# Six matrix jobs instead of four beside the first modulation, three of them summed in SBUF, and the later modulation loads spread out

## The reference, cut to what matters

```
mod = silu(c) @ w_ada + b_ada                      # 2048 x 12288 weights, one vector
sh_a, sc_a, gt_a, sh_f, sc_f, gt_f = split(mod, 6)
h = rmsnorm(x, norm_mix) * (1 + sc_a) + sh_a       # 256 x 2048
p = h @ w_in                                       # 2048 x 9296 weights
c_q, c_kv, k_pe, q_g, k_g, v_g, z, b_logit, a_logit, gates = split(p)
...                                                # attention from c_q, c_kv, k_pe; gated delta rule
                                                   # from conv(q_g, k_g, v_g); both gated and summed
```

## Time and profile before

| | |
|---|---|
| median of 3 runs | 2292.34 us (2292.03 to 2294.39) |
| the profiled execution | 2293.58 us, span 2292.3 us |
| PE busy | 2235.2 us (98%), mean granted clock 0.996 |
| PEld busy | 1855.7 us (81%) |
| DVE busy | 1505.7 us (66%) |
| ACT busy | 1009.0 us (44%) |
| DMA | 506.75 MB, 221 GB/s over the span; 363 and 381 GB/s in the first two fortieths |

### The profile page before, as it was taken

One profiled execution on the slowest core, in us unless ns is written; L12 is line 12 of the kernel. 1 busy time (PEld: TensorE's weight loads), 2 busy tenths in 40 slices (PEclk: granted clock), 3 DMA queues, 4 the chain that ended last, 5 costly groups with the idle time before them and its releaser, 6 DMA issues.

```text
span 2292.3 us, 26935 instructions
## 1 busy us (share of the span) xinstructions
PE 2235.2 (98%) x10767; PEld 1855.7 (81%) x10767; DVE 1505.7 (66%) x1927; ACT 1009.0 (44%) x1270; POOL 24.4 (1%) x28
## 2 busy tenths in 40 slices
PE   5998999999999999999999999999999999999998
PEld 3678898888887888888888888887888888888886
DVE  5888898887768777765554555467555555555556
ACT  4345445343444464443344434456444444434444
POOL 0000000000000000000000000000000000000000
PEclk9999999999999999999999999999999999999999
DMA  9966767685678768876555565555555555555553
GB/s 363 381 240 209 245 228 258 198 271 197 220 269 307 275 239 285 273 242 202 184 192 193 184 202 184 191 195 193 191 195 188 188 188 190 187 185 194 197 189 130
DMA packets 276445, 506.75 MB, mean 221 GB/s; under 512 B 24032, under 2 KB 38112, under 8 KB 275296
## 3 DMA queue, kind: packets, MB, share of 16 engines
q1 hardware_dynamic: 276320, 505.03, 65.0%
HBM read 502.51 MB, written 2.49 MB: 220 GB/s over the span
## 4 chain that ended last, share of the span: by engine, by line
PE 82%; DVE 8%; DMA 4%; ACT 2%; issue 2%; SPq 0%; POOL 0%; DVEq 0%; ACTq 0%
PE bank L1200 25%; PE bank L1202 25%; PE bank L1201 25%; DVE WL L1927 3%; PE bank L1391 2%; DMA RAW<-in_w_o_dram 2%; DVE GA L1908 1%; PE bank L1121 1%; ACT WH L1480 1%; PE bank L1212 1%; PE bank L1214 1%; PE bank L1213 1%; DMA RAW<-in_w_o_gdn_dram 1%; PE bank L1148 1%; PE bank L1363 1%
## 5 line engine op out<-in xcount | busy, mean ns | idle before, releaser
L1927 DVE TENSOR_TENSOR WL<-RAW,WH 128x1024 fp32r<-128x1024 f32 (+1 forms) x714 | 864.9, 1218 | 619.2 <-ACT WH L1480 616.5
L1480 ACT CAST WH<-RAW 128x1024 fp32r<-128x1024 f32 (+1 forms) x714 | 743.3, 1047 | 917.6 <-PE bank L1202 733.1
L1200 PE MATMUL bank<-WH,HTh 128*128 128x512 f32 x1936 | 770.4, 398 | 7.3 <-DVE WL L1927 6.5
L1202 PE MATMUL bank<-WH,HTl 128*128 128x512 f32 x1936 | 755.9, 390 | 0.0
L1201 PE MATMUL bank<-WL,HTh 128*128 128x512 f32 x1936 | 755.5, 390 | 0.0
L1200 PEld LDWEIGHTS bank<-WH,HTh 128*128 128x128 f32 x1936 | 364.2, 188 | 88.7 <-DVE WL L1927 11.3
L1201 PEld LDWEIGHTS bank<-WL,HTh 128*128 128x128 f32 x1936 | 364.4, 188 | 77.1 <-issue 4.3
L1202 PEld LDWEIGHTS bank<-WH,HTl 128*128 128x128 f32 x1936 | 364.0, 188 | 76.5
L1908 DVE SCALAR_TENSOR_TENSOR GA<-RAW,ST,GA 128x512 f32<-128x512 f32 x264 | 181.2, 747 | 13.9 <-DMA RAW<-in_w_ada_dram 7.7
L1200 PE MATMUL bank<-WH,R2h 128*128 128x512 f32 x408 | 164.1, 402 | 3.5 <-DVE WL L1927 3.5
L1202 PE MATMUL bank<-WH,R2l 128*128 128x512 f32 x408 | 159.9, 392 | 0.0
(11 more groups left out here) (273 smaller groups left out, 1756.3 us busy)
## 6 DMA issues: line engine op xcount, KB each, us to landing
RAW<-in_a_w_in_dram SPq DMA_DIRECT2D x96, 1024.0 KB, 5.0
RAW<-in_w_gate_up_dram SPq DMA_DIRECT2D x88, 1024.0 KB, 5.0
RAW<-in_w_ada_dram SPq DMA_DIRECT2D x80, 1024.0 KB, 5.2
RAW<-in_w_in_dram SPq DMA_DIRECT2D x63, 1024.0 KB, 5.0
RAW<-in_w_down_dram SPq DMA_DIRECT2D x44, 1024.0 KB, 5.0
RAW<-in_a_w_out_dram SPq DMA_DIRECT2D x32, 1024.0 KB, 5.0
A<-in_w_ada_dram SPq DMA_DIRECT2D x16, 1024.0 KB, 11.7
RAW<-in_w_o_dram SPq DMA_DIRECT2D x16, 1024.0 KB, 5.1
```

What stands on the lines that cost most here:

```text
L1200: e.matmul(o, ah[:, s], hi[:, k, :], start=first, stop=False)
L1202: i = e.matmul(o, al[:, s], hi[:, k, :], start=False, stop=last)
L1480: e.copy(hi, rv).then_inc(S["hi"], 1)
L1927: e.tensor_tensor(lo, rv, hi.bitcast(F32), ALU.subtract).then_inc(S["lo"], 1)
```

## The change

Two more jobs run in the front: `conv` 1 (here `q1`; `conv` 0 is `q0`) and the first gate job `ga` 0. The three jobs `q0`, `q1` and `ga` 0 share banks 6 and 7. Each runs its 4 kt of the round as a group of its own, and its partial sum is then taken to SBUF: in round 0 ACT copies it to a buffer CS, in the later rounds DVE adds it there (the new step `acc`, two instructions of 128x512, which wait for the end of that group). The order within a round becomes `cq`, `q0`, `ckv`, `q1`, `sm`, `ga`, with the g units between them. The final evictions of these three jobs read CS instead of PSUM. The rule that spreads the later g units is replaced by a table: none in `conv` 2 and the seven latent units, more in `ga`, `z` and `gb`. `JX` moves to another address.

The core of the diff:

```diff
@@ make_jobs
     front = [Job("sm", ...), Job("cq", ...), Job("ckv", ...),
-             conv(0, O_Q)]
-    a1 = [conv(1, O_Q + 512), conv(2, O_K)]
+             conv(0, O_Q), conv(1, O_Q + 512), Job("ga", 0, plain(win, O_GATE), 16, 512, "ht")]
+    for n in range(3):
+        front[3 + n].acc = n
+    a1 = [conv(2, O_K)]
@@ plan_units
-            w = [("w", j, 4 * c, 4) for j in jobs[:4]]
-            u.extend([w[0]] + f[:1] + [w[1]] + f[1:5] + [w[2]] + f[5:] + [w[3]])
+            sm, cq, ckv, q0, q1, ga = (("w", j, 4 * c, 4) for j in jobs[:6])
+            u.extend([cq] + f[:1] + [q0] + f[1:2] + [ckv] + f[2:3] + [q1] + f[3:5] + [sm] + f[5:6] + [ga] + f[6:])
...
-        thick = (("conv", 3), ("conv", 4), ("og", 2), ("og", 3))
+        quarters = {"conv": (0, 0, 0, 2, 2, 3), "ga": (0, 3, 3, 3), "z": (3, 3), "gb": (3, 3, 3, 3), "og": (1, 1, 2, 2), "wo": (2, 2, 0, 0),
+                    "uqn": (0, 0), "uqp": (0,), "ukk": (0, 0), "ukv": (0, 0)}
@@ front, one round c
             self.put("mod_e", 2 * c + 1, None)
             self.put("h", c)
+            if c:
+                self.front_unit()
+                self.put("acc", 2, c - 1, acc)
             if more:
                 self.front_unit()
             self.front_unit()
+            self.front_half(cq, 0)     # twice
...
+            self.front_half(q0, 3)     # twice
+            acc = self.used
+            if more:
                 self.front_unit()
             self.front_unit()
+            self.put("acc", 0, c, acc)
+            self.front_half(ckv, 1)    # twice
+            if more:
+                self.front_unit()
+            self.front_half(q1, 3)     # twice
+            acc = self.used
+            if more:
+                self.front_unit()
+            self.front_unit()
+            self.put("acc", 1, c, acc)
+            if more:
+                self.put("mod_e", 2 * c + 2, None)
+                self.put("cam", c + 1)
+                self.front_unit()
+            else:
+                self.put("rope_tables")
+            self.front_unit()
+            if more:
                 self.front_unit()
                 self.front_unit()
+            self.front_half(sm, 2)     # twice
+            self.front_half(ga, 3)     # twice
+            acc = self.used
+        self.put("acc", 2, 3, acc)
@@ pe_program, half
+            group = j.nkt if j.acc is None else 4
...
-                first, last = kt == 0, kt == j.nkt - 1
+                first, last = kt % group == 0, kt % group == group - 1
@@ act_program
+        elif kind == "acc" and args[1] == 0:
+            n, _, done = args
+            W.wait_ge("half", done)
+            for q in range(2):
+                e.copy(L.CS[n][:, 512 * q:512 * q + 512], bank[6 + q]).then_inc(S["acc_a"], 1)
@@ dve_program
+        elif kind == "acc" and args[1]:
+            n, c, done = args
+            W.wait_ge("half", done)
+            W.wait_ge(*acc_event(n, c - 1))
+            for q in range(2):
+                total = L.CS[n][:, 512 * q:512 * q + 512]
+                e.tensor_tensor(total, bank[6 + q], total, ALU.add).then_inc(S["acc_d"], 1)
```

More of the change, by code:

```diff
@@ L461, in front @@
         self.issue_loads()
-        where = {"cq": 0, "ckv": 1, "conv": 3, "sm": 2}
+        sm, cq, ckv, q0, q1, ga = jobs
         for ci in range(2):
@@ L482, in front @@
             self.front_unit()
-            for j in (jobs[0], jobs[1]):
-                self.front_halves(j, where[j.name])
-            for _ in range(4 * more):
+            self.front_half(cq, 0)
+            self.front_half(cq, 0)
+            if more:
+                self.front_unit()
+            else:
+                latent = self.done(cq, 0)
+                next(latent)
+            self.front_unit()
+            self.front_half(q0, 3)
+            if not more:
+                next(latent)
+            self.front_half(q0, 3)
+            acc = self.used
+            if more:
                 self.front_unit()
             self.front_unit()
-            self.front_halves(jobs[2], where[jobs[2].name])
+            self.put("acc", 0, c, acc)
+            self.front_half(ckv, 1)
+            if not more:
+                next(latent, None)
+            self.front_half(ckv, 1)
+            if more:
+                self.front_unit()
+            self.front_half(q1, 3)
+            self.front_half(q1, 3)
+            acc = self.used
[6 more added lines that the diff above has]
+                self.put("cam", c + 1)
+                self.front_unit()
+            else:
+                self.put("rope_tables")
+            self.front_unit()
             if more:
@@ L518, in front_unit, with front_half @@
         self.issue_loads()
-    def front_halves(self, j, where):
-        for _ in range(2):
-            self.put("half", self.used, where)
-            self.used += 1
+    def front_half(self, j, where):
+        assert self.halves[self.used][0] is j
+        self.put("half", self.used, where)
+        self.used += 1
         j.end = self.used
@@ L779, in q_rest, with first_convs @@
         self.have.add("qpt")
+    def first_convs(self):
+        for n in range(2):
+            for i in range(2):
+                self.put("conv", n, i, None)
+                yield
+            self.bg.append(self.conv_rest(n))
+            yield
+            yield
     def conv_rest(self, n):
@@ L1188, in pe_program @@
                 b, pr = (bank[2 * where], bank[2 * where + 1]), (where,)
-            if t0 == 0 and tiles[0] == 0:
+            group = j.nkt if j.acc is None else 4
+            if t0 % group == 0 and tiles[0] == 0:
                 for n in pr:
@@ L1218, in pe_program @@
                 i.then_inc(S["tile"], 1)
-            if t0 + nk == j.nkt:
+            if (t0 + nk) % group == 0:
                 for n in pr:
-                    held[n] = evicted(j)
+                    held[n] = evicted(j) if j.acc is None else [acc_event(j.acc, t0 // 4)]
         elif kind == "lat_t":
@@ L1598, in act_program @@
                 W.wait_ge(*RAW1_FREE[1])
-            W.wait_ge("half", job_end(sch, "conv", n))
+            if n < 2:
+                W.wait_ge(*acc_event(n, 3))
+                u = [L.CS[n][:, 512 * q:512 * q + 512] for q in range(2)]
+            else:
+                W.wait_ge("half", job_end(sch, "conv", n))
+                u = [bank[2 * pr], bank[2 * pr + 1]]
             W.wait_ge("nat_t", 2 * n - 2)
@@ L1653, in act_program @@
             W.wait_ge("att_lo", 8)
-            W.wait_ge("half", job_end(sch, kind, c))
+            if (kind, c) == ("ga", 0):
+                W.wait_ge(*acc_event(2, 3))
+                u = [L.CS[2][:, 512 * bb:512 * bb + 512] for bb in range(2)]
+            else:
+                W.wait_ge("half", job_end(sch, kind, c))
+                u = [bank[2 * pr], bank[2 * pr + 1]]
             d = L.M if kind == "ga" else L.GB
             for bb in range(2):
-                e.activation(d[:, bb, 512 * c:512 * c + 512], bank[2 * pr + bb], ACT.Tanh, scale=0.5
+                e.activation(d[:, bb, 512 * c:512 * c + 512], u[bb], ACT.Tanh, scale=0.5
                              ).then_inc(S[kind], 1)
```

47 lines of the change are left out of this document (27 added, 20 removed).

## The result

The changed kernel takes 2365.99 us (2365.71 to 2368.9, 4 runs) against 2293.36 us (2292.03 to 2294.58, 4 runs) beside it: ratio 1.0319, 95% interval 1.0306 to 1.0332. It is slower, as forecast, but by 73 us where 39 were forecast, and 2366 is outside the range of 2312 to 2350.

A forecast was written before the change was run, and what follows sets the result against it. It took DMA to bound the front, DVE the stage behind, TensorE 340 to 680 us. Front stalls 38.7, clock +9, small waits -1, stage behind -10, stage after +2 gave +38.7 us: 2331 us, range 2312 to 2350.

The forecast's parts named there:

- The chain behind `q1`: In the front, PE waits for DVE's ordered work after the group of `q1`; stalls together 38.7 us (36.5 to 40).
- The bounds on an `acc`: DVE's adding step in the front was taken as 1.4 us, between 1.1 and 1.5 us.
- The clock: PE runs at half clock after each long front stall: 9 us taken, 5 to 17 possible.
- Small waits in the front: PE's earlier mid-round gaps for g units in the front go: -1 us (-3 to 0).
- rival 1: Front runs as its loads say, PE's 5.8 us lack there gone: -14 us, 2278 us; chance 6%.
- The stage behind the front: From 155.6 to 340 us before, fewer g units relieve DVE and PE waits less: -10 us (-16 to 0).
- on average PE leads: Behind the front, some 129 us of DVE work would stand against 148 us of PE work.
- The stage after it: 340 to 680 us: 11 more g units in `b1`, 30 us of DVE, cost PE +2 us (0 to +10).
- Rival 3: DVE becomes the bound in `b1` on top of the front's stalls: +62 us, 2354 us; chance 9%.

The follow-up runs named there:

- the third kernel: Changed kernel with only the front reordered: g units, `mod_e` and rope tables ahead of the `acc` they stood behind; new table kept; 2316.71 us.
- kernels 1 and 2: First: changed kernel with the old g-unit rule, `gb` 0 and 1 thick, 2358.76 us; second: kernel before with the new table alone, 2300.3 us.
- Kernel 6 against 5: Five front jobs, reordered front, old rule, `gb` 0 thick: 6 has `conv` 1 there without `ga` 0, 2310.03 us; 5 the reverse, 2301.81 us.
- Kernel 9: `kp` put two slots later, against six front jobs in the reordered front with the old g-unit rule (2312.27 us); 2312.25 us.
- kernel 8: VectorE's taps on `conv` 0 and 1 narrowed to 16 columns, against six jobs, reordered front, old rule (2312.27 us); 2306.55 us.
- kernels 10 and 11: `ga` 3 instead of `ga` 2 without g units: 10 with six jobs and `kp` later, 2307.58 us; 11 with five jobs including `ga` 0, 2295.46 us.
- kernel 7: Six jobs, reordered front, new table with three g units moved from `ga` 2 and 3 to `conv` 4, 5 and `gb` 0; 2314.35 us.

## Why the prediction was wrong, point by point

The forecast was +38.7 us, and the two steps that failed are its terms for what comes behind the front: -10 for the stage behind it and +2 for the stage after that. Measured, they are +6.7 and +27.5 us. The front was 7.8 us cheaper than forecast, which hid part of it.

**The chain behind `q1`: right.** Forecast 11.0 us in rounds 1 and 2, 7.2 in round 0, 6.9 in round 3, 2.6 at the end, 38.7 in all. The trace has 10.7 twice, 7.3, 6.7 and 2.5 (PE in order of time; the first two of them):

```profile
80.22 3.78 PE L1201 MATMUL bank<-GA,CST 128*128 128x512 f32 x4 [7.25 <-DVE GA L1982]
...
132.73 3.78 PE L1201 MATMUL bank<-GA,CST 128*128 128x512 f32 x4 [10.67 <-DVE GA L1982]
```

An `acc` took 1.29 us, within its bounds of 1.1 to 1.5. Rounds took 50.5, 53.6 and 52.3 us; 53 was forecast. (The bounds on an `acc`, which stands in four of the five sums, give 37.5 to 39.1, not 36.5 to 40.)

**The clock: right in kind, a little less.** The account has 9.7 us of slow clock in the front against 2.6 before, so 7.1 where 9 was taken. The forecast's lower end of 5 came from no row (five stalls at 1.7 us are 8.5). The front of after has 41 us at half clock; 9.7 us lost to it means that some 20 of them had PE at work, and the others lay within the waits, where they cost nothing. The Trainium skill ("TensorE: Matmul & The Clock Gate", section "Loop structure matters more than you think") has VectorE's copy out of PSUM as something that does not break PE's warmth where the next matmuls follow at once. The traces agree with that condition: in the third kernel, with the same `acc` beside matmuls that go on, the clock is full from 46.4 to 227.3 us; in after PE stood for VectorE, and the clock fell to half at each long wait.

**Small waits in the front: too small.** Forecast -1 us (-3 to 0). Before lost 18.5 us to `conv` 2, 2.6 of it by the clock, so 15.9 by waits; after has 57.4 - 9.7 = 47.7, of which 37.8 are the five named. That leaves 9.9, 6.0 less, of which 2.0 with its clock are `conv` 1's own, lost behind the front before. The prediction had such a sum itself, as the 5.8 us in rival 1, but not in the main sum. `conv` 2 so began at 240.84 us, not at 247.

**The stage behind the front: the first step that failed.** Forecast -10 us (-16 to 0), measured 24.7 - 18.0 = +6.7 (+4.7 if `conv` 1's 2.0 us are counted here, as the prediction did). The waits for VectorE that were to become fewer went from 15.3 to 18.1 us, and the slow clock from 2.8 to 6.6. The part on g units was right: kernels 1 and 2 show the table worth -11 to -13 us there. (By the rule in `plan_units` 17 g units stood in `a1`, two of them in `conv` 1, where 18 and four were counted; that is 2.7 us of VectorE and moves no term.) What failed is the other half of the sentence, that `conv` 1's 23 us of PE work go and only 9.4 us of splits with them, so that "on average PE leads". The average was the wrong measure. The jobs from `conv` 2 to `conv` 3 have beside them the taking out of `conv` 0, `conv` 1, `conv` 2, both latents and `sm`'s gates (PE loses 17.9 us there, 9.9 before), and VectorE was already nearly full there before, 43.65 of 46.9 us from `uqn` 0 to `conv` 3 (the kernel before, columns as above):

```profile
212.50:259.40 46.90, 43.63 (x281) 39.42 (x282) 43.65 (x71) 25.16 (x36) 4.22 (x4) 0.96 0.82 238
```

`conv` 1's PE work was the cover for that. Kernel 6 against 5 prices it at 20 us, of which the table hides 11 to 13. Kernel 9 shows that the one place tried is not to blame, and kernel 8 that the loss answers in part to VectorE's load: 3.4 us for 7.

**The stage after it: the second step that failed, and the larger miss.** Forecast +2 (0 to +10), measured 20.9 from `ga` 1 to `z` 0 and 10.0 from `z` 0 to `og` 2, less 3.4 in the rest: +27.5. Here too the sum went by the average load (87% of VectorE over 340 us) and named no "dense stretch". Two can be named. `ga` 3 now holds the inverse with three g units (VectorE 25.07 of 26 us; kernels 10 and 11 take 4.7 and 6.3 us away by freeing it, with the old rule's two units; how much of after's 20.9 us it is was not measured by itself, kernel 7 with half the units gone moved 9). And before `og` 2 the sum of a chunk waits for a late VectorE, in all four kernels with a new table (after, 2, 3 and 7; 5.0 to 5.7 us) and in none of the others.

**Rival 3** (VectorE becomes the bound in `b1`, nothing gained behind the front, 2354 us, given 9%) named what happened beyond the chain. Its sum was 38.7 + 10 + 13 = 62; measured, the parts are 38.9 for front and clock, and 34 behind, with the stage behind the front not at zero but 6.7 us worse than before. Its 2354 us are still 12 short.

Of after's 72 us (the spans differ by 72.4), the runs so show: 39 in the front, 47 to 49 against the same six jobs in another order; 18 to 20 by moving `conv` 1, 5 by moving `ga` 0, and the table, which returns 11 to 13 behind the front and takes 15 to 16 from `ga` 1 to `z` 0 (9 in the kernel before) and 7 to 9 from `z` 0 to `og` 2. Why the attention's waits change between 3.1 and 5.7 us when the same steps shift by a few halves stays open.

## What to carry to other kernels

Before moving work out of a stage, ask what it covers there. Here VectorE was busy for 93% of the stretch from `uqn` 0 to `conv` 3, and of the 23 us of TensorE's work that were taken away ahead of it, 20 came back as waits and slow clock. In a kernel whose side steps are counted in units of the main work, taking a unit out also slides every later step to another neighbour: list where the steps with many small instructions fall before and after. And when a wait disappears by moving one instruction, look two steps later before counting it as won.
